# Where the mixer's b and k vectors are scaled, and how its first 64x64 blocks are masked and completed

## The reference, cut to what matters

```python
kk = kk / jnp.maximum(jnp.sqrt(jnp.sum(kk * kk, axis=-1, keepdims=True)), 1e-12)
a_vec = -kk
b_vec = kk * ah
def step(S, inp):
    r_t, w_t, k_t, v_t, a_t, b_t = inp
    sa = jnp.einsum('bhvk,bhk->bhv', S, a_t)
    S = S * w_t[:, :, None, :] + sa[..., None] * b_t[:, :, None, :] + v_t[..., None] * k_t[:, :, None, :]
    return S, jnp.einsum('bhvk,bhk->bhv', S, r_t)
```

## Time and profile before

| | us |
|---|---|
| median of 3 runs | 2538.95 (2538.88 to 2540.92) |
| the profiled execution's own time | 2538.88 |
| its span, first to last instruction | 2537.1 |
| mixer stage, 201 to 516 in the span | 315 |
| TensorE busy in the whole span | 2397.6 (95%) |
| VectorE, ScalarE, GpSimd busy | 1531.8, 947.2, 627.4 |

### The profile page before, as it was taken

How to read it: one execution, slowest core, us unless ns; L and a number is a source line. 1 busy time by engine, 2 the same in 40 slices (tenths; PEclk the granted TensorE clock), 3 DMA queues, 4 the chain that set the end, 5 groups by cost and what they waited for, 6 DMA issues and landing times. The chain is left out here.

```text
span 2537.1 us, 50332 instructions
## 1 busy us (share of the span) xinstructions
PE 2397.6 (95%) x20078; PEld 2344.0 (92%) x20078; DVE 1531.8 (60%) x2819; ACT 947.2 (37%) x1802; POOL 627.4 (25%) x304
## 2 busy tenths in 40 slices
PE   7995888878999998999899999999999999999997
PEld 6994777777999998999899999999999999999997
DVE  4244666434889885999455544554455445777774
ACT  4235555223333336999532222222222222222221
POOL 2432354322455552111222112211221120000000
PEclk9997999779999999999999999999999999999999
DMA  4431000031333333777733233323332333555451
GB/s 179 130 105 56 27 27 15 1 137 45 108 104 103 108 121 97 223 216 212 237 135 120 96 100 107 120 94 101 109 120 93 101 112 100 172 169 178 164 181 43
DMA packets 162477, 296.03 MB, mean 117 GB/s; under 512 B 11888, under 2 KB 99248, under 8 KB 158136
## 3 DMA queue, kind: packets, MB, share of 16 engines
q1 hardware_dynamic: 162360, 294.38, 35.4%
HBM read 230.03 MB, written 64.31 MB: 116 GB/s over the span
## 5 line engine op out<-in xcount | busy, mean ns | idle before, releaser
L124 PE MATMUL banks<-w_high,v_low 128*128 128x288 f32 x2048 | 604.3, 295 | 0.0
L122 PE MATMUL banks<-w_high,v_high 128*128 128x288 f32 x2048 | 603.7, 295 | 0.4
L123 PE MATMUL banks<-w_low,v_high 128*128 128x288 f32 x2048 | 602.9, 294 | 0.0
L122 PE MATMUL banks<-res_hi,u_high 128*128 128x288 f32 x1440 | 437.6, 304 | 7.2 <-POOL u_low L1708 6.6
L123 PE MATMUL banks<-res_lo,u_high 128*128 128x288 f32 x1440 | 425.6, 296 | 0.0
L124 PE MATMUL banks<-res_hi,u_low 128*128 128x288 f32 x1440 | 425.6, 296 | 0.0
L122 PEld LDWEIGHTS banks<-w_high,v_high 128*128 128x128 f32 x2048 | 384.1, 188 | 3.7 <-DVE w_low L2111 3.7
L2135 DVE TENSOR_TENSOR res_x<-banks,res_x 128x288 f32<-128x288 f32 x512 | 225.2, 454 | 267.1 <-PE banks L124 267.1
L124 PEld LDWEIGHTS banks<-w_high,v_low 128*128 128x128 f32 x2048 | 384.2, 188 | 0.0
L123 PEld LDWEIGHTS banks<-w_low,v_high 128*128 128x128 f32 x2048 | 384.1, 188 | 0.0
L1708 POOL TENSOR_TENSOR u_low<-u_raw,u_high 128x1024 fp32r<-128x1024 f32 x71 | 181.5, 2556 | 692.2 <-ACT u_high L1704 692.1
(11 more groups left out here) (337 smaller groups left out, 4214.5 us busy)
## 6 DMA issues: line engine op xcount, KB each, us to landing
v_raw<-arg_v SPq DMA_DIRECT2D x128, 512.0 KB, 3.9
scratch_gates<-gate_stage SPq DMA_DIRECT2D x18, 2048.0 KB, 9.5
gates_in<-scratch_gates SPq DMA_DIRECT2D x32, 1152.0 KB, 7.2
u_raw<-arg_u SPq DMA_DIRECT2D x35, 1024.0 KB, 5.8
q_raw<-arg_u SPq DMA_DIRECT2D x38, 512.0 KB, 3.6
scratch_hidden<-gelu_ahead SPq DMA_DIRECT2D x56, 288.0 KB, 2.4
gelu_out<-scratch_hidden SPq DMA_DIRECT2D x56, 288.0 KB, 2.9
in_raw<-arg_w_in SPq DMA_DIRECT2D x25, 512.0 KB, 3.9
```

The costliest lines, as they stand in the source:

```text
L122: pe.matmul(out, ah, bh, start=first, stop=False)
L123: pe.matmul(out, ah, bl, start=False, stop=False)
L124: return pe.matmul(out, al, bh, start=False, stop=last)
```

## The change

Three things change together.

1. `tmp_a`, `b_hat` and `k_hat` move on VectorE from part A5 to the end of part A3. The semaphore `hats` now counts b, k, a, r, and TensorE and ScalarE handle the four transposes in that order; the blocks `ab` now come before `m`. ScalarE's B5 waits for the next tile's second hat instead of its third.
2. The identity is no longer added by one VectorE operation of 768 columns for each half. VectorE adds it to mT in an operation of 256 columns, and gets the transposed inverse from mT with a mask that now holds the diagonal. The first inverse gets its identity from GpSimd, in a new part B1.
3. `ab` is masked once for each half, not twice. Level 1 on TensorE waits for two semaphores in the place of one. The tile `mT_inv_blocks` is split in two, `mT_blocks` and `inv_blocks`.

```diff
-            c[:, C_LTB:C_LTB + HALF_T] = high
+            c[:, C_LTB:C_LTB + HALF_T] = high | (s == t)
...
-            "B1": [("aT", "act"), ("rT", "act"), ("bT", "act"), ("kT", "act")]
-                  + [(f"{name}{e}", "dve") for name in ("m", "ab") for e in range(2)]
+            "B1": [("bT", "act"), ("kT", "act"), ("aT", "act"), ("rT", "act")]
+                  + [(f"{name}{e}", "dve") for name in ("ab", "m") for e in range(2)]
...
 TensorE, b1
-                    b.wait_taken(pe, "bT", i)
-
+                    b.wait_taken(pe, "aT", i)
+
+                    blocks("ab", i, T, bT, aT)
                     blocks("m", i, T, aT, bT)
-                    blocks("ab", i, T, bT, aT)
...
 TensorE, s1 and s2
-                    b.wait_taken(pe, "kT", i)
                     scores("ak", i, T, kT, aT)
 
                 def s2(i, tok, T, rc, xc):
+                    b.wait_taken(pe, "rT", i)
                     scores("rb", i, T, bT, rT)
...
 TensorE, level 1
-                                pe.wait_ge(first_rdy, 2 * i + e + 1)
+                                pe.wait_ge(x_rdy, 2 * i + e + 1)
+                                pe.wait_ge(xt_rdy, 2 * i + e + 1)
...
 GpSimd
+                def b1(i, tok, T, rc, xc):
+                    b_fence(pool, i)
+                    for e in range(2):
+                        b.wait_taken(pool, f"m{e}", i)
+                        x = inv[0:T, e, 0]
+                        TT(x, x, bc(cst[0:T, C_IDB:C_IDB + HALF_T], 1, [T, 4, HALF_T]), ALU.add).then_inc(x_rdy, 1)
...
 VectorE, a3 (at its end) and a5
+                    link(TT(t0[0:T], kk[0:T], h3(wa[0:T, 1, :]), ALU.mult))
+                    b.wait_taken(dve, "cinc", i)
+                    TT(h3(bh2[0:T, i % 2, :]), t0[0:T], eneg[0:T], ALU.mult).then_inc(hats, 1)
+                    TT(h3(kh2[0:T, i % 2, :]), km[0:T], eneg[0:T], ALU.mult).then_inc(hats, 1)
...
-                    link(TT(t0[0:T], kk[0:T], h3(wa[0:T, 1, :]), ALU.mult))
-                    b.wait_taken(dve, "cinc", i)
-                    TT(h3(bh2[0:T, i % 2, :]), t0[0:T], eneg[0:T], ALU.mult).then_inc(hats, 1)
-                    TT(h3(kh2[0:T, i % 2, :]), km[0:T], eneg[0:T], ALU.mult).then_inc(hats, 1)
...
 VectorE, b1
                     for e in range(2):
+                        in_blocks(f"ab{e}", i, T, mT[0:T, e], C_MSB)
+                    for e in range(2):
                         in_blocks(f"m{e}", i, T, inv[0:T, e, 0], C_LEV)
+                    b.wait_taken(dve, "ab1", i)
                     for e in range(2):
-                        o = b.get(dve, f"ab{e}", i)[0:T, 0:4 * HALF_T].rearrange("p (q t) -> p q t", t=HALF_T)
-                        TT(mT[0:T, e], o, block_mask(C_MSB, T), ALU.mult).then_inc(first_masked, 1)
-                        b.took(TT(inv[0:T, e, 1], o, block_mask(C_LTB, T), ALU.mult), f"ab{e}", i)
-                        dve.wait_ge(first_masked, 2 * i + e + 1)
-                        b.wait_taken(dve, f"ab{e}", i)
-                        x = m_inv[0:T, e].rearrange("p x q t -> p (x q) t")
-                        TT(x, x, bc(cst[0:T, C_IDB:C_IDB + HALF_T], 1, [T, 12, HALF_T]), ALU.add).then_inc(first_rdy, 1)
+                        link(TT(mT[0:T, e], mT[0:T, e], block_mask(C_IDB, T), ALU.add))
+                        TT(inv[0:T, e, 1], mT[0:T, e], block_mask(C_LTB, T), ALU.mult).then_inc(xt_rdy, 1)
```

More of the change, by code:

```diff
@@ L665, in mix @@
         hats = core.sem("hats")
-        first_masked, first_rdy = core.sem("first_blocks_masked"), core.sem("first_blocks_ready")
+        mt_rdy = core.sem("mT_ready")
+        x_rdy, xt_rdy = core.sem("inv_first"), core.sem("invT_first")
         s0d_rdy = core.sem("s_mid_pairs_ready")
@@ L865, in b1 @@
                     b_fence(pe, i)
-                    for n, (name, src) in enumerate((("aT", ah), ("rT", rh), ("bT", bh2[:, i % 2]), ("kT", kh2[:, i % 2]))):
+                    for n, (name, src) in enumerate((("bT", bh2[:, i % 2]), ("kT", kh2[:, i % 2]), ("aT", ah), ("rT", rh))):
                         pe.wait_ge(hats, 4 * i + n + 1)
@@ L1072, in b1 @@
                     b_fence(act, i)
-                    for name, dst in (("aT", aT), ("rT", rT), ("bT", bT), ("kT", kT)):
+                    for name, dst in (("bT", bT), ("kT", kT), ("aT", aT), ("rT", rT)):
                         take(name, i, dst[:, :, 0:T], 4 * T)
@@ L1112, in b5 @@
                     if i + 1 < NT:
-                        act.wait_ge(hats, 4 * (i + 1) + 3)
+                        act.wait_ge(hats, 4 * (i + 1) + 2)
                     take("y", i, ys[0:T], 512)
```

7 lines of the change are left out of this document (3 added, 4 removed).

## The result

The changed kernel takes 2574.89 us (median of 4 runs, 2570.71 to 2583.89), against 2539.93 for the kernel before on the same chip: a ratio of 1.0136, 95% interval 1.0112 to 1.0161. That is 35 us slower. The forecast was 2561.1 in a range of 2548 to 2571, so the sign and the place were right and the size was too small. The profiled execution took 2569.98 us, span 2567.9.

A forecast was written before the change was run, and what follows sets the result against it. TensorE was taken to set the pace in the mixer stage, whose losses pass on one for one. Move 14.7, B1 2.0 and clock 5.5 make 22.2 us on 2538.88: 2561.1 us, range 2548 to 2571.

The forecast's parts named there:

- TensorE's clock: Behind level 4's standstill TensorE drops to 1.2 GHz: 5.5 us over three tiles, bounds 0 and 14.4.
- the two places of 0.56 and 7.39 us: VectorE's slack before level 4 is 0.56 us; after part A5 it idles 7.39; three operations go from the second to the first.
- The price of the moved operations: Before level 4, VectorE takes turns with GpSimd: 4.5 us of new standstill in a tile, 14.7 over four tiles.
- Nothing comes back in A5.: After part A5: the 4.6 us it gets shorter become VectorE idle time before the state product, no gain.
- Start and order of transposes: In front of the first tile and at the hats' transposes: the new order costs nothing, both set at 0.
- Part B1: Before level 1: GpSimd's additions and tmp_c compete with VectorE; +0.4 us per tile, +2.0 in all, ends -5.5 and +2.5.
- The stall, but not the clock: Rival: TensorE stands still before level 4 but stays at 2.4 GHz, B1 near zero or better; 2551.6 us, chance 0.22.
- The clock stays low longer: Rival: each standstill costs the rest of the tile at half rate in three tiles; about 2580 us, chance 0.08.
- I am wrong if the wait in front of level 1 shrinks: Sign of error: TensorE's wait there shrinks by more than half a microsecond, so GpSimd's part of B1 is free.
- The range: 2548 to 2571 us for the whole kernel, leaving out the tail of the long low clock.

The follow-up runs named there:

- gated: The changed kernel with GpSimd's output scaling (C3) held until VectorE has signalled the next tile's k_hat: 2569.01 us, 1.0122.
- move_only: The kernel before with only the move of the three operations and the new order of transposes, B1 as it was: 2563.91 us, 1.0084.
- b1_only: The changed kernel with tmp_a, b_hat and k_hat back in part A5; B1 and the order of transposes stay as changed: 2558.3 us, 1.0062.
- after_tmpc: The changed kernel, move kept, with only GpSimd's tmp_c put in front of its two additions of the identity: 2560.88 us, 1.0080.
- tmpc_first: The run b1_only with GpSimd's tmp_c put in front of its additions of the identity: 2538.78 us, 0.9994 of the kernel before.
- busy_after2: The changed kernel with idle TensorE products, results unread, sized to end inside its longer waits in the mixer and output projection: 2553.93 us, 1.0047.
- b1_busy: The run b1_only with idle TensorE products in its two waits before level 1 alone: 2552.53 us, 1.0053 of the kernel before.

## Why the prediction was wrong in size

The step that failed is the term of TensorE's clock: I charged the lower level only for the standstill at level 4, 5.5 us, and nothing of it for part B1. What the profile shows there is 21.4 us of new busy time for the same matmuls. The idle time, which I had summed to 16.7 us (14.7 + 2.0), grew by 9.4, so a part of that error was offset by another.

- **What bounds the kernel; the two places of 0.56 and 7.39 us.** Right. The loss lies wholly in the mixer stage and passed on one for one.
- **The price of the moved operations, 4.5 us.** Right: 4.62, 4.62 and 4.81 us in the second to fourth tile, and `gated` shows that the cause is turns with GpSimd (0.69 us each without it, 1.64 to 1.75 with it). In the fourth I had taken 3.7 and it was 4.81; what I had subtracted came back one level later, where the wait fell from 1.44 to 0.58. In the first I took 2.0 and it was 0.99: `rkT`'s masks came 0.02 us too late to meet L1361, and in `move_only` they met, with 2.42. That the sum of the waits is 15.0, against 14.7, is in part luck.
- **"Nothing comes back in A5."** Right: VectorE's idle time before the state product went from 7.39 to 14.22 us in the second tile and 18.19 in the third. I had said some 4 more; it is 6.8 in the second, since the operations left in A5 no longer take turns with GpSimd either (L1297, `r_hat`, 0.69 us in place of 1.75), and in the third the low stretch from 410 makes it 10.8.
- **Start and order of transposes, 0.** TensorE starts 2.65 us earlier, at 226.25, on `b_hat`, but then waits for `a_hat` and runs at the lower level; level 1 starts at 236.5 in place of 236.0. Right for the sum.
- **Part B1, +2.0 with ends of -5.5 and +2.5. Here the step failed most.** The order of events was as I had it (`tmp_c` between the halves, the second half late), and the waits of a full tile at the higher clock grew by 0.6 us in place of 0.4. But the half of the change costs 16 us alone (`b1_only`) and 14 together with the move (`after_tmpc`). I had priced B1 in idle time only, and asked for the clock only at level 4. `tmpc_first` shows that `tmp_c` behind the additions is all of it. That it works through the clock is read from the profiles: the same matmuls took 13.7 us longer in a tile of `b1_only`, with no more idle time than before (this in its slowest execution, 50 us above before, where the median's loss is 16).
- **TensorE's clock, 5.5 us.** For the move alone about right on the median: 21 us measured, where the profile has 14.8 of new idle time (but 13.2 of new busy time, in an execution of 2566.82). It fell behind each long wait at level 4, as said (0.56 at 396.8). For the whole change it was too small by far: 21.4 us of new busy time, with 9.4 of idle time. And it lay elsewhere than I had put it: at 410 and at the next tile's start, far behind the wait, and for 71.7 us from the last tile into the output projection, where the kernel before has 44.4.
- **The rivals.** "The stall, but not the clock" (2551.6) is refuted by the changed kernel, but is near what `busy_after2` measures, 2553.93, with a higher clock (and with the last waits of the stage filled too). "The clock stays low longer" (2580, 0.08) was nearest in kind and got too small a chance. "I am wrong if the wait in front of level 1 shrinks": it grew, 1.64 to 2.33.
- **The range.** Its upper end, 2571, left out the tail of the low clock. One program's executions lie up to 37 us apart with the clock (`b1_only`), which the three runs of before, within 2 us, did not let me see. Of the changed kernel 24 executions are on record, 2569.49 to 2589.32, and ten of them lie inside the range.

Open: what brings the lower level on. It is not the single wait (2.34 us in `tmpc_first` leaves 1.00), and not the sum of the idle time (138.3 us in `b1_only` and in `tmpc_first`). How `tmp_c` between the halves, which adds one wait of 0.96 us to a tile, brings it on is not shown; filling that wait in `b1_busy` did not settle it. Nor is it shown why `b1_only` gave 2554 in one execution and 2591 in another.

## What to carry to other kernels

Before moving an operation, look up the slack of the place it goes to, and what the other engine that shares its memory runs beside it: three operations of 0.69 us cost 4.6 us in a place with 0.56 us of slack and a busy GpSimd. An experiment that empties that place must hold the neighbour back by a wait; deleted work is followed by the next work in the queue. And where TensorE sets the pace, price each new gap twice, once as idle time and once as clock, and widen the range by the spread that the clock makes.

## What the runs showed of the hardware that I had not expected

- The granted clock can halve with TensorE at work nearly all the time: 25.04 us busy of 27.30 at 0.51, in the window shown of `b1_only`. In the first 5.60 us of it, from 278.40, TensorE is busy throughout at 0.50, and the longest wait of the 30 us before is 1.28 us.
- The place of one GpSimd operation of 1.22 us changed the time by some 17 us (1.0062 to 0.9994 of the kernel before), and by 14 us in another version of the kernel, with no more idle time of TensorE.
- Work whose result nobody reads can make a kernel faster: 2574.89 to 2553.93 us. Much the same filling gave the kernel before nothing on the median (1.0013 [0.9985, 1.0041]).
- L1363, which reads a bank, keeps its 0.42 us behind an L1361 that GpSimd stretches to 1.48; an addition of 256 columns between SBUF tiles goes from 0.41 to 1.26. The Trainium skill (GPSIMD Engine Reference, Specifications) tells of such contention for instructions with two SBUF inputs, and these rows agree.
